# Latent attention with stacked position queries, zero-padded position keys and a position key product whose columns are streamed four times

## What is computed

```python
h = x @ w_in                                   # 2048 -> 512 (c_q) + 512 (c_kv) + 64 (k_pe) + 2048 (z)
q = (rms_norm_2(c_q, q_norm) @ w_uq)           # 16 heads x (128 + 64)
q_nope, q_pe = q[..., :128], apply_rope(q[..., 128:], cos, sin)
k_pe = apply_rope(k_pe, cos, sin)              # 64 numbers a token, shared by all heads
kv = (rms_norm_2(c_kv, kv_norm) @ w_ukv)       # 16 heads x (128 k_nope + 128 v)
s = (q_nope . k_nope + q_pe . k_pe) * (128 + 64) ** -0.5   # per head, masked to k <= q
o = softmax(s) @ v
y = (o * silu(z)) @ w_out
x = layer_norm(alpha * x + y)
```

## Time and profile before

| | us |
|---|---|
| median of 3 runs | 3686.37 (3684.34 to 3688.64) |
| span of the profiled execution | 3686.1 |
| PE busy | 3289.0 (89%) |
| POOL busy | 2205.7 (60%) |
| DVE busy | 1670.4 (45%) |
| ACT busy | 1334.9 (36%) |

### The profile page before, as it was taken

The page is one execution under the profiler, slowest core; times in us unless marked ns, Lnnn a source line. Parts: engine busy times, 40 slices in busy tenths (PEclk is TensorE's granted clock), DMA queues, the critical chain, the costliest instruction groups (busy, mean ns, idle before and its releaser), DMA issues.

```text
span 3686.1 us, 38752 instructions
## 1 busy us (share of the span) xinstructions
PE 3289.0 (89%) x13658; PEld 2324.8 (63%) x13658; DVE 1670.4 (45%) x2526; ACT 1334.9 (36%) x2017; POOL 2205.7 (60%) x1224
## 2 busy tenths in 40 slices
PE   8999999994787788777777789999999999989997
PEld 6888778883343243233232348888888888868886
DVE  7998154217665448445644542232223222321342
ACT  5777575452111011010100014444444444444553
POOL 3021767886444544454545438788778877866665
PEclk9999999997999999999999989999999999989998
DMA  7455544659999999999999965555545555544444
GB/s 217 135 149 142 163 141 160 222 172 351 419 419 420 422 419 421 421 421 419 421 417 422 421 238 177 169 174 174 170 170 174 175 170 168 169 161 140 135 137 148
DMA packets 231691, 936.75 MB, mean 254 GB/s; under 512 B 28000, under 2 KB 31072, under 8 KB 164960
## 3 DMA queue, kind: packets, MB, share of 16 engines
q0 software_dynamic: 76288, 538.74, 35.3%
q1 hardware_dynamic: 151776, 391.96, 32.8%
q10 hardware_dynamic: 3456, 3.75, 0.3%
HBM read 927.02 MB, written 2.10 MB: 252 GB/s over the span
## 4 chain that ended last, share of the span: by engine, by line
PE 55%; DMA 24%; POOL 10%; issue 5%; DVE 4%; ACT 1%; DVEq 1%; POOLq 0%; ACTq 0%; SPq 0%
PE products L675 32%; DMA arena<-peer_up_in,arena 20%; PE products L1343 9%; POOL weights_low L618 8%; PE products L1875 7%; DMA arena<-peer_down_in,arena 4%; POOL arena L1820 2%; DVE arena L1829 1%; PE products L1094 1%; PE products L2421 1%; PE products L2383 1%; PE products L1200 1%; PE products L1117 1%; PE products L1379 0%; PE products L1441 0%
## 5 line engine op out<-in xcount | busy, mean ns | idle before, releaser
L618 POOL TENSOR_TENSOR weights_low<-arena,weights_high 128x1024 fp32r<-128x1024 f32 x496 | 1218.8, 2465 | 407.6 <-ACT weights_high L606 406.6
L1875 PE MATMUL products<-arena 128*128 128x512 f32 x1984 | 941.1, 619 | 314.5 <-DMA arena<-peer_up_in,arena 233.0
L606 ACT ACTIVATE weights_high<-arena 128x1024 fp32r<-128x1024 f32 x612 | 646.5, 1059 | 1012.2 <-PE products L675 995.1
L675 PE MATMUL products<-weights_high,input_high 128*128 128x512 f32 x2432 | 992.6, 408 | 10.8 <-DVE weights_low L618 5.5
L675 PE MATMUL products<-weights_low,input_high 128*128 128x512 f32 x2432 | 954.2, 392 | 0.0
L675 PE MATMUL products<-weights_high,input_low 128*128 128x512 f32 x2432 | 952.5, 392 | 0.0
L1875 PEld LDWEIGHTS products<-arena 128*128 128x128 f32 x1984 | 370.5, 195 | 868.2 <-issue 451.2
L1829 DVE SCALAR_TENSOR_TENSOR arena<-arena 128x2048 f32<-128x2048 f32 x256 | 586.1, 2292 | 523.7 <-DMA arena<-peer_down_in,arena 523.1
L1820 POOL DMA_INDIRECT arena<-peer_up_in,arena x256 | 380.9, 1488 | 531.5 <-PE products L1875 507.5
L675 PEld LDWEIGHTS products<-weights_high,input_high 128*128 128x128 f32 x2432 | 459.7, 189 | 107.4 <-issue 14.8
L675 PEld LDWEIGHTS products<-weights_low,input_high 128*128 128x128 f32 x2432 | 458.6, 189 | 99.7
(11 more groups left out here) (325 smaller groups left out, 2976.7 us busy)
## 6 DMA issues: line engine op xcount, KB each, us to landing
arena<-dsa_in SPq DMA_DIRECT2D x320, 512.0 KB, 3.5
arena<-w_in_in SPq DMA_DIRECT2D x128, 512.0 KB, 3.8
arena<-mla_wide_in SPq DMA_DIRECT2D x97, 512.0 KB, 3.5
arena<-w_attn_o_in SPq DMA_DIRECT2D x32, 512.0 KB, 4.2
arena<-w_out_in SPq DMA_DIRECT2D x32, 512.0 KB, 4.6
arena<-peer_w_query_in SPq DMA_DIRECT2D x32, 512.0 KB, 4.5
arena<-dsa_w_out_in SPq DMA_DIRECT2D x32, 512.0 KB, 3.7
arena<-glu_w_b_in SPq DMA_DIRECT2D x16, 512.0 KB, 3.5
```

Of the source, the lines that this page charges most:

```text
L606: nc.scalar.activation(w_hi[:, u % RING, :, at], ring[:, u % RING, :, at], ACT.Copy).then_inc(hi_made, 1)
L618: ops.tensor_tensor(w_lo[:, u % RING, :, at], ring[:, u % RING, :, at], w_hi[:, u % RING, :, at].bitcast(F32), op=ALU.subtract).then_inc(l ...
L675: mm = nc.tensor.matmul(PS[:, bank(b) + t, 0:width], x[:, x0 + n, at], y, start=n == 0 and m == 0, stop=n == len(parts) * PK - 1 and m == 2)
L1875: mm = nc.tensor.matmul(PS[:, SUM_BANKS[q]], diag[:, d % ROWS], row[:, q * NC:(q + 1) * NC], start=h % 2 == 0 and n == 0, stop=bool(last))
```

## The change

Three things are changed, all in the latent attention.

- **The `kpe` product.** The moving operand of its 96 matmuls is the same 64 columns, read four times over (a broadcast dimension), so each is 256 columns wide and writes four copies of the result side by side. Only the first 64 columns are used.
- **Stacked queries.** `QPM` holds the two heads of a pair one above the other: partitions 0 to 63 the first, 64 to 127 the second. The `qpe` turn is two transposes of 128 x 128 instead of four of 128 x 64, and ACT copies 128 partitions x 256 instead of 64 x 512.
- **Padded keys.** `KPE` is now two matrices of 128 partitions: the first has the position keys on partitions 0 to 63 and zeros below, the second zeros above and the keys on partitions 64 to 127. The score product of a head multiplies all 128 rows of `QPM` with the matrix of its half; the other head's rows meet zeros. For this DVE clears `KPE` (one memset), rotates the keys into the first of two copies of their rows and copies them to the second, PE turns both copies at once, and ACT copies the two halves out with two instructions.

```diff
@@ -246,6 +246,7 @@
 MLA_PAIRS = HEADS // 2
 UQ_W = 2 * (HD + ROPE_B)
 UP_PARTS = QR // (PK * P)
+KPE_WIDE = 4
 
 
 def mla_order():
@@ -504,9 +505,9 @@
         ln_gain = arena[:, WIDTH - 2 * D:WIDTH - D]
         ln_shift = arena[:, WIDTH - D:WIDTH]
         cols = Columns(arena, second, WIDTH)
-        kpe_rows = cols.take(NT, ROPE_B)
-        KPE = cols.take(SEQ)
-        QM, QPM, KM = cols.take(2, 2, SEQ), cols.take(2, 2, SEQ), cols.take(2, 2, SEQ)
+        kpe_rows = cols.take(NT, 2, ROPE_B)
+        KPE = cols.take(2, SEQ)
+        QM, QPM, KM = cols.take(2, 2, SEQ), cols.take(2, SEQ), cols.take(2, 2, SEQ)
         qpe_rows = cols.take(2, NT, 2, ROPE_B)
         VM = cols.take(2, NT, 2, HD)
         PM = cols.take(2, NT, SEQ)
@@ -1340,7 +1341,11 @@
                 for t in range(NT):
                     q = slice(t * P, (t + 1) * P)
                     for m, (x, y) in enumerate(((xh, hi), (xl, hi), (xh, lo))):
-                        mm = nc.tensor.matmul(PS[:, 2 * side + t, 0:width], x[:, x0 + PK * u + k, q], y,
+                        to = PS[:, 2 * side + t, 0:width]
+                        if kind == "kpe":
+                            to = PS[:, 2 * side + t, 0:KPE_WIDE * ROPE_B].rearrange("p (a n) -> p a n", a=KPE_WIDE)
+                            y = y.unsqueeze(1).to_broadcast([P, KPE_WIDE, ROPE_B])
+                        mm = nc.tensor.matmul(to, x[:, x0 + PK * u + k, q], y,
                                               start=u == 0 and k == 0 and m == 0, stop=last and k == tiles - 1 and m == 2)
             mm.then_inc(parts_used, 1)
 
@@ -1360,7 +1365,7 @@
                 src = [rows2[:, 1, t, k * P:(k + 1) * P] for k in (2 * j, 2 * j + 1) for t in range(NT)]
             elif kind == "kpe":
                 pe.wait_ge(rows2_ready, DSA_ROPES + 1)
-                src = [kpe_rows[:, t] for t in range(NT)]
+                src = [kpe_rows[:, t].rearrange("p a e -> p (a e)") for t in range(NT)]
             elif kind == "z":
                 if j % 2 == 0:
                     mla_emptied(pe, "z", j // 2)
@@ -1370,13 +1375,13 @@
                 src = [rows2[:, 1, t, k * P:(k + 1) * P] for k in (0, 1) for t in range(NT)]
             elif kind == "qpe":
                 pe.wait_ge(rows2_ready, DSA_ROPES + 2 + j)
-                src = [qpe_rows[:, j % 2, t, h] for h in (0, 1) for t in range(NT)]
+                src = [qpe_rows[:, j % 2, t].rearrange("p h e -> p (h e)") for t in range(NT)]
             else:
                 mla_emptied(pe, "ukv", j)
                 src = [rows2[:, 1, t, k * P:(k + 1) * P] for k in (2, 3) for t in range(NT)]
             pe.wait_ge(turned, after(x - 1))
             for b, block_ in enumerate(src):
-                nt = nc.tensor.transpose(PS[0:block_.shape[1], M_TURN_BANK, b * P:(b + 1) * P], block_, ident)
+                nt = nc.tensor.transpose(PS[:, M_TURN_BANK, b * P:(b + 1) * P], block_, ident)
             nt.then_inc(turn_ready, 1)
 
         def mla_turn_act(act, n):
@@ -1392,13 +1397,16 @@
                     hi = nc.scalar.activation(CHR[:, k0 + k], two[:, k], ACT.Copy, scale=vec[:, 34 + k0 + k:35 + k0 + k])
                 hi.then_inc(turned_hi, 1)
             elif kind == "kpe":
-                nc.scalar.activation(KPE[0:ROPE_B], PS[0:ROPE_B, M_TURN_BANK, 0:SEQ], ACT.Copy).then_inc(turned, 1)
+                for half in range(2):
+                    at = slice(half * ROPE_B, (half + 1) * ROPE_B)
+                    kp = nc.scalar.activation(KPE[at, half], PS[at, M_TURN_BANK, 0:SEQ], ACT.Copy)
+                kp.then_inc(turned, 1)
             elif kind == "z":
                 nc.scalar.activation(ZM[:, 2 * j:2 * j + 2], two, ACT.Copy).then_inc(turned, 1)
             elif kind == "q":
                 nc.scalar.activation(QM[:, j % 2], two, ACT.Copy).then_inc(turned, 1)
             elif kind == "qpe":
-                nc.scalar.activation(QPM[0:ROPE_B, j % 2], two[0:ROPE_B], ACT.Copy).then_inc(turned, 1)
+                nc.scalar.activation(QPM[:, j % 2], two[:, 0], ACT.Copy).then_inc(turned, 1)
             else:
                 nc.scalar.activation(KM[:, j % 2], two, ACT.Copy).then_inc(turned, 1)
 
@@ -1438,8 +1446,8 @@
                     q = slice(t * P, (t + 1) * P)
                     nc.tensor.matmul(PS[:, M_SCORE_BANK, at:at + seen], QM[:, buf, half, q], KM[:, buf, half, 0:seen],
                                      start=True, stop=False)
-                    mm = nc.tensor.matmul(PS[:, M_SCORE_BANK, at:at + seen], QPM[0:ROPE_B, buf, half, q],
-                                          KPE[0:ROPE_B, 0:seen], start=False, stop=True)
+                    mm = nc.tensor.matmul(PS[:, M_SCORE_BANK, at:at + seen], QPM[:, buf, q], KPE[:, half, 0:seen],
+                                          start=False, stop=True)
                     at += seen
                 mm.then_inc(score_made, 1)
             if k == 4:
@@ -1566,8 +1574,11 @@
                     nc.vector.tensor_scalar(rows2[:, r, t], mla_bank(which, 0)[:, t], full_inv[:, t:t + 1], None,
                                             ALU.mult).then_inc(evac[r], 1)
             if n == 17:
-                rope(dve, mla_bank("kpe", 0)[:, :, 0:ROPE_B].unsqueeze(2), kpe_rows.unsqueeze(2), cos_b, sin_b,
-                     ROPE_B // 2, evac[0], 2, lambda: mla_made(dve, "kpe", 0, 0)).then_inc(rows2_ready, 1)
+                nc.vector.memset(KPE, 0.0)
+                rope(dve, mla_bank("kpe", 0)[:, :, 0:ROPE_B].unsqueeze(2), kpe_rows[:, :, 0:1], cos_b, sin_b,
+                     ROPE_B // 2, evac[0], 2, lambda: mla_made(dve, "kpe", 0, 0))
+                dve.drain()
+                nc.vector.tensor_copy(kpe_rows[:, :, 1], kpe_rows[:, :, 0]).then_inc(rows2_ready, 1)
             for h, k in mla_heads(n):
                 mla_head_dve(dve, h, k)
             mla_turn_dve(dve, n)
```

## The result

The changed kernel takes 3661.8 us in the median of 5 runs (3660.3 to 3663.2), against 3684.5 us of the kernel before, now 5 runs (3681.5 to 3688.6). The ratio is 0.9938, with a 95% interval of 0.9927 to 0.9948: 22.7 us faster, between 19 and 27. The gain forecast was 20.4 us.

What follows compares the result with a forecast made beforehand. PE was taken to bound the kernel in the heads' stretch. Savings of 11.8 + 1.8 + 4.2 + 2.6 = 20.4 us off the 3686.1 us span gave 3665.7, plus 0.3 for the median: 3666.0 us, range 3662 to 3678.5.

Steps and rivals of the forecast that it cites:

- The bound: Latent attention heads: PE's own list ends last, busy 233.3 of 234.8 us, so an edit gains what it takes off PE.
- Scores: Score products of 16 heads: 128 rows throughout remove late loads, 0.74 us a head, 11.8 us in all.
- the row count: Score products: each change between 128 and 64 rows, four a head, makes a weight load start late.
- Turns: Query transposes: two fewer in each of 8 pairs at 0.11 us each, saving 1.8 us.
- Position product: Position key's 96 matmuls at 256 columns: 12.0 us instead of 16.2 with the clock staying at 1.00, saving 4.2 us.
- the price at 256 columns: Position key's product: 0.125 us a matmul, drawn from 512-wide parts at 0.229 and a 384-wide one at 0.177.
- the 2.6 us behind: First 13 `z` matmuls after the position product: at the high clock 3.0 us instead of 5.6, saving 2.6 us.
- Sum: Whole kernel: the four savings together take 20.4 us off the profiled span of 3686.1 us.
- The fallen clock: Rival, position product: clock falls despite wide matmuls, nothing gained in `z`, 12.9 us left, 3673.5 us; chance 0.12.
- the float32 rate: Rival, position product: 256 columns take 0.43 us a matmul, kernel 8.9 us slower, 3695.3 us; chance 0.09.
- The padding: Rival, scores: padding doesn't remove the wait, scores keep 2.04 us, gain only 8.6 us, 3677.8 us; chance 0.08.
- The partial loss: Rival, heads' stretch: 5 us of PE's gain given back waiting for softmax or ACT's copies, 3671 us; chance 0.10.

Runs made afterwards that it cites:

- e3: Kernel before with position products of the scores zero-padded to 128 rows, queries not stacked, position key's product still 64 columns wide; 3671.8 us.
- e7: Kernel before with position products of the scores padded to 96 rows instead of 128, not stacked; 3670.3 us.
- e2: Changed kernel with the position key's product back at 64 columns a matmul; 3671.1 us.
- e6: Changed kernel with the position key's columns streamed twice, 128 columns a matmul, instead of four times; 3661.3 us.
- e10: Changed kernel with high and low weight parts side by side, 64 position key matmuls of 128 columns instead of 96; 3660.3 us.

## Why the prediction was right or wrong

**The bound.** Right. PE was the last in the heads' stretch, and what was taken from it came off the end. PE's waits there are what they were, one of 0.3 us, so nothing was given back to the softmax.

**Scores, 11.8 us.** Right in place, 0.5 us too small: e3 alone gained 12.3 at 1.00 (13.4 as measured). Part of that is what follows the scores: I charged 0.15 us behind every head, which is right before a turn. Where a product part follows, it costs 0.19. The chain behind the third head's scores, first in the kernel before, then in the changed one:

```profile
3422.05 2.28 PE products L1343 x12
```

```profile
3407.46 2.09 PE products L1348 x12
```

The cause as I put it, the row count, was too wide (e7).

**Turns, 1.8 us.** Right: 0.22 instead of 0.44 us, and 2.0 between e3 and e2 (1.7 at 1.00).

**Position product, 4.2 us.** It was 4.7 by the traces, 16.2 - 11.5. The term was mis-sized by the price at 256 columns: 0.120 us instead of 0.125. The straight line through 384 and 512 columns would have given it. The 384-wide part that I took had 2.12 us, another one, at 3471.56 in the same chain, has 2.09, and from 2.09 the line gives 0.119. The clock held, and the 2.6 us behind came out at 2.6: 13 `z` matmuls in 3.0 us instead of 5.6.

**Sum.** It was 20.4 us against 20.6 in the layer, the mean of two traces of each. That it fits so closely is in part luck: in two other traces the low clock was 3.4 us shorter than in both of the kernel before, and from one like them the change would have gained 1.6 us less.

**The time and its range.** This is the step that failed: "11.8 + 1.8 + 4.2 + 2.6 = 20.4 us off the profiled span of 3686.1, so 3665.7; the median stands 0.3 us above the span", with a range that began at 3662. The cost of the change was not what failed; the base was. It amounts to the median of three runs, 3686.4, less 20.4. Five runs put that median at 3684.5, so the base was 1.9 us too high, and from 3684.5 the same sum gives 3664.1. And the agreement with the span was chance. In all runs that list both numbers the time lies 1.8 to 2.4 us above the execution's own span (3661.8 and 3660.0; 3685.04 and 3683.2), so the profiled execution of before lasted some 3688 us and was one of the slower ones.

The rest of the miss is 2.3 us: 22.7 between the medians against 20.4. The two traces of each kernel show 20.6 in the layer, and the interval of the gain, 19 to 27 us, holds that. The medians of the unchanged kernel alone came out between 3682.9 and 3686.4 in this work. So the 2.3 us can be the spread of the runs; no run shows another source, and whether there is one stays open. I had built the range from the costs of the change alone. Its lower end sat 4 us under the forecast, less than the 7 us over which runs of the unchanged kernel spread, and the time fell 0.2 us outside it.

**The rivals.** The fallen clock and the float32 rate would have been seen in the rows of the product, and weren't. The padding did what it was for. The partial loss would have been seen in PE's waits, and they didn't grow.

## What to carry to other kernels

Look in the chain for matmul pieces that cost more than the same shape elsewhere, and then at the loads: one that starts together with its own matmul was not hidden. Small contractions among full ones were cheaper padded, here already with 96 rows, or put next to each other. When two traces are compared, take the time at the low clock out of both first: here it moved a layer by up to 1.6 us that had nothing to do with the change. And when a forecast rests on one profiled execution, take the spread of the runs into the range before any cost of the change.

## What the runs showed of the hardware that I had not expected

- A matmul of 96 rows beside one of 128 pays nothing, one of 64 rows 0.15 to 0.20 us at each change, and two of 64 in a row nothing.
- In a full queue of matmuls the granted clock fell from 1.00 to 0.50 when they were 64 columns wide (seven traces), and stayed at 1.00 when they were 128 wide (three), 256 (three) or 512 (one). The pace was nearly the same at the first three widths: 0.1125, 0.111 and 0.120 us.
- Once fallen, the clock stayed at 0.50 for 13.6 us in two traces and for 17.1 us in five, past the end of the 64-wide product.
- Behind the expert layer, where PE waits for transfers, the granted clock over 85 us was 0.92 to 0.96, and the first product there started at 2168.8 us in e6, 2170.3 in the kernel before and 2172.5 in e10. The last layer starts up to 10 us apart in executions of programs that are the same up to there.
